# Two-layer encoder trunk, one core: the last branch's output product taken by groups of four PSUM banks

## What is computed

```python
ga, gb, gc = jnp.split(jax.nn.sigmoid(pg), N_BRANCH, axis=-1)
merged = ga * (ya @ w_proj_a[i]) + gb * (yb @ w_proj_b[i]) + gc * (yc @ w_proj_c[i])
h = h + merged @ w_out[i]
```

## Time and profile before

| | us |
|---|---|
| median of 3 runs | 2196.46 |
| lowest and highest | 2194.92, 2198.64 |
| the profiled execution's own time | 2196.55 |
| its span in the trace | 2194.8 |

### The profile page before, as it was taken

The page is one execution under the profiler, slowest core; times in us unless marked ns, Lnnn a source line. Parts: engine busy times, 40 slices in busy tenths (PEclk is TensorE's granted clock), DMA queues, the critical chain, the costliest instruction groups (busy, mean ns, idle before and its releaser), DMA issues.

```text
span 2194.8 us, 36156 instructions
## 1 busy us (share of the span) xinstructions
PE 2109.9 (96%) x15316; PEld 1831.8 (83%) x15316; DVE 1466.7 (67%) x1323; ACT 1230.4 (56%) x1144; POOL 22.5 (1%) x24
## 2 busy tenths in 40 slices
PE   9999889999999999998998999999999999999997
PEld 7877779999999787787997888888888888888886
DVE  5633337554443763334746889898888888889894
ACT  4454354344332445445426777777777777777673
POOL 0000100000000000010000000000000000000000
PEclk9999999999999999999999999999999999999998
DMA  6332105434443232211435989889898989989892
GB/s 242 116 96 99 56 3 192 154 124 184 159 187 137 77 116 97 77 41 41 178 130 196 377 337 363 356 347 367 341 368 337 370 333 369 356 345 375 331 376 86
DMA packets 73839, 484.89 MB, mean 221 GB/s; under 512 B 12424, under 2 KB 13576, under 8 KB 15992
## 3 DMA queue, kind: packets, MB, share of 16 engines
q1 hardware_dynamic: 69960, 478.62, 56.7%
q10 hardware_dynamic: 3760, 4.52, 0.7%
HBM read 481.36 MB, written 1.74 MB: 220 GB/s over the span
## 4 chain that ended last, share of the span: by engine, by line
PE 88%; DVE 6%; ACT 3%; issue 1%; DMA 1%; ACTq 0%; DVEq 0%; SPq 0%
PE PS L499 22%; PE PS L501 22%; PE PS L500 22%; PE PS L895 5%; PE PS L761 2%; DVE area L1664 2%; PE PS L779 2%; DVE WL L1664 2%; PE PS L1115 1%; PE PS L1122 1%; PE PS L640 1%; ACT WH L1578 1%; DMA ring<-in_experts 1%; PE PS L803 1%; PE PS L554 1%
## 5 line engine op out<-in xcount | busy, mean ns | idle before, releaser
L1664 DVE TENSOR_TENSOR WL<-ring,WH 128x2048 fp32r<-128x2048 f32 x414 | 943.6, 2290 | 280.4 <-ACT WH L1242 166.9
L1578 ACT ACTIVATE WH<-ring 128x2048 fp32r<-128x2048 f32 x336 | 642.9, 1916 | 173.7 <-PE PS L501 139.7
L499 PE MATMUL PS<-WH,XGH 128*128 128x512 f32 x896 | 355.4, 397 | 4.4 <-DVE XGL L1664 4.2
L501 PE MATMUL PS<-WL,XGH 128*128 128x512 f32 x896 | 350.5, 391 | 0.0
L500 PE MATMUL PS<-WH,XGL 128*128 128x512 f32 x896 | 350.0, 391 | 0.0
L1242 ACT ACTIVATE WH<-ring 128x2048 fp32r<-128x2048 f32 x78 | 149.0, 1910 | 139.6 <-PE PS L501 139.5
L501 PE MATMUL PS<-XL,WH 128*128 128x272 f32 (+1 forms) x704 | 203.2, 289 | 0.0
L499 PEld LDWEIGHTS PS<-WH,XGH 128*128 128x128 f32 x896 | 168.8, 188 | 40.9 <-DVE XGL L1664 4.4
L501 PEld LDWEIGHTS PS<-WL,XGH 128*128 128x128 f32 x896 | 168.7, 188 | 36.1
L500 PEld LDWEIGHTS PS<-WH,XGL 128*128 128x128 f32 x896 | 169.0, 189 | 33.5
L499 PE MATMUL PS<-WH,HTH 128*128 128x512 f32 x448 | 176.6, 394 | 0.6
(11 more groups left out here) (328 smaller groups left out, 3562.7 us busy)
## 6 DMA issues: line engine op xcount, KB each, us to landing
ring<-in_experts SPq DMA_DIRECT2D x336, 1024.0 KB, 6.8
ring<-in_weights SPq DMA_DIRECT2D x114, 1024.0 KB, 6.9
ring<-in_weights SPq DMA_DIRECT2D x4, 576.0 KB, 6.2
ring<-in_weights SPq DMA_DIRECT2D x4, 512.0 KB, 4.1
cst<-in_consts ACTq DMA_DIRECT2D x1, 1731.0 KB, 8.7
area<-in_x ACTq DMA_DIRECT2D x2, 512.0 KB, 4.8
out<-area SPq DMA_DIRECT2D x4, 256.0 KB, 2.2
bias_line<-lin SPq DMA_DIRECT2D x1, 672.0 KB
```

What stands on the lines that cost most here:

```text
L499: pe.matmul(o, lh, rh, start=first, stop=False, skip_group_check=True)
L501: return pe.matmul(o, lh, rl, start=False, stop=last, skip_group_check=True)
L1578: act.activation(WH[(BASE + j) % 3][:, :], ring[b][:, 2048 * (j % 2):2048 * (j % 2) + 2048], ACT.Copy).then_inc(S("w_hi"), 1)
L1664: tt = lambda o, a_, b_, op: dve.tensor_tensor(o, a_, b_, op)
```

## The change

A new function `rows_by_banks` does P1 in both layers, in place of the two calls of `rows_half`. It takes banks 0 to 3 through both weight halves first (24 matmuls with half 12, 24 with half 13), gives `m_p`, and then banks 4 to 7 through both. `w_used` is given for each half within the second group. The order of the six matmuls into a bank with one weight half is as before. On ScalarE `merged_high(0)`, and on VectorE `gated(2, 0)` and `merged_low(0)`, are hung one half earlier: behind the making of half 14, ahead of half 15. P0 and P2 are as they were.

```diff
+            def rows_by_banks(l, name, lo, xh, xl, before, mid):
+
+                g = split_half[(l, name)]
+                for group in range(2):
+                    for half in range(2):
+                        wh, wl = half_ready(g + half)
+                        if half == 0:
+                            before(4 * group)
+                        for d_ in range(4 * group, 4 * group + 4):
+                            for i in range(2):
+                                k, c = 2 * half + i, slice(i * D + d_ * P, i * D + d_ * P + P)
+                                ins = three_products(PS[:, d_, lo:T], wh[:, c], wl[:, c], xh(k), xl(k), k == 0, k == 3)
+                        if group:
+                            ins.then_inc(S("w_used"), 1)
+                    if group == 0:
+                        ins.then_inc(S(mid), 1)
...
                     y_lo = [YL[0], YL[1][:, :, PADC:TP], YL[2]][b]
+                    if j == 2:
+                        rows_by_banks(l, f"P{b}", lo, lambda k: YH[b][:, k, lo:], lambda k: y_lo[:, k, lo:],
+                                      lambda d_: pe.wait_ge(S("m_s"), at("m_s", l, 4 + d_ // 4)), "m_p")
+                        continue
...
                 for h in range(2):
-                    after_half(events, l, f"P{MERGE_ORDER[2]}", 1).append((merged_high, h))
+                    after_half(events, l, f"P{MERGE_ORDER[2]}", h).append((merged_high, h))
...
                     for h in range(2):
-                        after_half(events, l, f"P{b}", 1).append((gated, j, h))
+                        after_half(events, l, f"P{b}", 1 if j < 2 else 0).append((gated, j, h))
                         if j == 2:
-                            after_half(events, l, f"P{b}", 1).append((merged_low, h))
+                            after_half(events, l, f"P{b}", h).append((merged_low, h))
```

## The result

| | before | changed |
|---|---|---|
| median of 9 runs each | 2194.92 | 2183.90 |
| lowest and highest | 2191.94, 2209.50 | 2181.97, 2190.59 |
| the profiled execution: own time, span | 2196.55, 2194.8 | 2184.36, 2182.5 |
| mean granted clock over the span | 0.983 | 0.987 |

The ratio is 0.9945, 95% interval 0.9929 to 0.9962: 12.1 us faster, between 8.3 and 15.6.

The account below looks back on a forecast made before the run. TensorE was taken to bound the kernel, through its waits for `ML` and the low clock behind them. Gains of 3.99 and 3.81 us, 7.8 together, from 2196.55 gave 2188.7 us, range 2185.8 to 2192.3.

Parts of the forecast that it names:

- What bounds the kernel: TensorE paces the kernel; it waits 6.9 us for `ML`, once per layer, and a low clock follows each wait.
- The first chain: Merge steps before O0's first half: hidden behind P1's second group, ready 0.6 and 0.5 us early, removing layer 0's 3.56 us stall.
- the price of 0 for the permutation: Reordering P1's matmuls itself costs nothing, bounded at 0.1 us a layer either way.
- rival D: P1's second weight half comes too late and stops P1, one us per us of lateness, about 2201; chance 0.02.
- rival E: TensorE still waits for the first chain at O0's start, 0.5 us a layer, 2190.5; chance 0.05.
- The second chain: Merge steps before O0's second half: late behind low half 15, new stalls 1.18 and 1.44 us, gains 3.99 and 3.81 us.
- The clock behind a short wait: After the new stalls before O0's second half the clock stays up: cost 0, with 1.6 us a layer for the range.
- the row of 1.47 us: A dense-stage stall with granted clock 1.00 behind it, the evidence that the new stalls would not lower the clock.
- So I see nothing that stands still while the rest moves up: All work after each layer's O1 moves up with TensorE, so the full 0.36% should be measured.
- The term for low clock elsewhere: Low-clock stretches elsewhere might be shifted away, each worth 1.6 us; chance 0.05 of more gain than summed.
- rival C: The wait only changes place and part of the gain is taken back further on, 2191.5 or 2192.6; chance 0.10.
- The range: For the whole kernel's median time: 2185.8 to 2192.3 us, around a forecast of 2188.7.

Follow-up runs that it names:

- experiment 3: Kernel before with only the new order of P1's matmuls; gatings and merge steps hang where they hung before: ratio 1.0050 to the kernel before, 11.0 us slower.
- experiment 4: Kernel before with only the events moved one half earlier, P1 by rows as before: ratio 0.9989 to the kernel before.
- experiment 2: Changed kernel with `gated(2, 1)` hung behind half 15, as the prediction assumed: ratio 0.9983 to the kernel before, 3.7 us faster.
- experiment 5: The whole change in layer 0 alone, layer 1 as before: ratio 0.9976 to the kernel before, 5.3 us faster.
- experiment 6: The whole change in layer 1 alone, layer 0 as before: ratio 0.9976 to the kernel before, 5.3 us faster.
- experiment 8: The kernel before, unchanged, timed and traced again: ratio 1.0001.
- experiment 9: The changed kernel, unaltered, timed a third time beside the kernel before: ratio 0.9945.
- experiment 1: The changed kernel, unaltered, timed again beside the kernel before: ratio 0.9963, 8.1 us faster.
- the reciprocal: VectorE's `spread(0)` moved behind the first branch's gating: ratios to the kernel before 0.9930 and 0.9956 on the changed kernel, 0.9983 on the kernel before.

## Why the prediction was right or wrong

**What bounds the kernel: right.** The 6.9 us of wait and the low clock behind it were what the change had to win, and went. Experiments 3 and 4 show that neither half of the change does it alone.

**The first chain: right.** It was to start at 408.82 with TensorE's slot at 414.64; the product began 6.22 us after P1's start, as said (408.38 - 402.16 and 408.82 - 402.60), and O0 started 12.05 us after P1 in layer 0 and 11.37 in layer 1. P1 took as long as before, so the price of 0 for the permutation holds. The second weight half at a quarter of P1 (rival D) and the late first chain (rival E) cost nothing.

**The second chain: wrong, by a misreading.** The step "low half 15 at 414.41 ... `gated(2, 1)` begins at 416.62" took the gating of the second half to be hung behind half 15. In the code it is hung behind half 14. So it starts when P1 ends, 12.25 us after P1's start instead of 14.02, and the low half fills the time in which ScalarE rounds. The chain itself is longer, since the subtraction waits for VectorE until 419.14, but TensorE gets it 18.41 instead of 19.24 us after P1's start. Experiment 2 has the order that was assumed and its trace gives the assumed numbers to 0.03 us, so it is this step and no duration that failed. It accounts for 9.5 - 7.8 = 1.7 us.

**The clock behind a short wait: right, on thin ground.** No fall behind 1.00 and 1.30 us of idle time in the one trace that has them (experiment 2), as the row of 1.47 us said; in the changed kernel itself the waits are 0.15 and 0.36 us, and the question hardly arises. The Trainium skill ("TensorE: Matmul & The Clock Gate", section "A second HAM failure mode: psum-queue depth-cycling") tells of short gaps between groups that came often enough to make the clock oscillate; the single gap in each layer of experiment 2 did not lower it. The row of 1.47 us was a sound one: that wait and two of 1.43 us in the dense stage have 1.00 behind them in all fourteen traces. But the trace that the prediction was made from also has the wait of 1.94 us with 0.58 behind it (experiment 4), and the prediction does not weigh it. At 1.9 and 2.2 us it went both ways, at 3.4 us it fell each time, for longer or shorter: S in the unchanged order was 23.24 and 24.41 in layer 0, and 22.28, 22.10 and 23.50 in layer 1, by that alone.

**"So I see nothing that stands still while the rest moves up": right, but it missed the noise.** The term for low clock elsewhere was set at 0 with 1.6 us of range. The first pair of traces differs by 2.7 us outside the two stages. Experiments 5, 6, 8 and 9 show no effect of the change there: between the layers the changed kernel took 671.4, 671.0 and 674.0 us, the kernel before 673.4 and 669.5. Nor is anything of the gain taken back behind (rival C): from O1 of layer 1 to the last matmul it is 1056.8, 1055.3 and 1055.8 against 1057.2 and 1054.6. O1 itself starts 6.12 and 5.72 us after O0's second half, 6.05 and 5.69 before, so the later weight halves held nothing up. The three ratios of the changed kernel, 0.9945, 0.9963 and 0.9945, average 0.9951 or 10.8 us, and the 9.5 us (0.9957) of the two stages lie within all three intervals. Why the mean lies 1.3 us above them was not settled; it is less than the width of each interval.

**The range** was built from the mechanism's bounds alone. The measured 2183.9 is 4.8 us below the forecast. The misread step is 1.7 of them. Another 1.6 are the starting point: the forecast subtracts from 2196.55, one execution, and the median of nine executions of the kernel before was 2194.92. The last 1.5 were not settled; they are less than the 4 us by which the ratios of one and the same kernel differed (0.9945 and 0.9963). With the misread step alone set right the forecast would have been 2187.1, and a range shifted with it (2184.1 to 2190.6) would still have missed.

## What to carry to other kernels

Where an engine's work is queued by hand, a chain of small steps between two products is worth moving ahead of the preparation of later weights, but only if the product's order also gives the chain its input early: here the matmul order alone lost 7.3 us in the two stages of its trace (11 as timed), the queue order alone gave 4.0 (nothing that the timing could tell), and both together gave 9.5 (about 11 as timed). Read each moved event's place from the expression in the diff, index by index, and write the resulting order of the engine down before summing; here one missing `h` made the kernel 1.7 us faster than its description. A wait that looks like a dependence may be an unrelated instruction queued ahead of the one waited for: look at what the releasing engine did just before it, as with the reciprocal.

## What the runs showed of the hardware

**The clock goes with much of the spread of this one-core program.** In experiment 1 the execution with a mean granted clock of 0.988 took 2183.3 us and the one with 0.981 took 2197.2, which is 2.0 us for each thousandth. A mean that is a thousandth lower over 2195 us is 4.4 us more at the lower level, or 2.2 us of lost work, which is that size. The relation is loose, though: a line through all the executions gives 1.8 us for each thousandth in experiment 1 (without the one of 7347 us), but 0.7, 1.5 and 1.1 in the three sets of the kernel before that were timed beside the experiments (29, 29 and 23 executions), and 2.6 in experiment 2. In the traces of experiment 8 the first 403 us became 10 us longer while the number of matmuls and the work of the other engines stayed the same; only the clock differed (0.95 and 0.98).

**A lower clock can follow a wait of about 2 us or not**, for the same kind of matmuls behind it (experiment 4: 1.00 and 0.77 after 2.25 and 2.17 us; 0.58 and 1.00 after 1.94 and 1.96 us of one and the same kernel), so a price for it should be kept as a range. Length alone doesn't decide: at 757.50 us of the kernel before, after a wait of 1.71 us ahead of which TensorE ran matmuls of 32 rows, the next 4.0 us have a granted clock of 0.50, while the waits of 1.43 and 1.47 us in the dense stage have 1.00 behind them.
